# Three of every four FFN-up pairs by seven half-size products, with new orders on all queues

## The chip, the cores and the metric

The kernel runs on one core of one Trainium2 chip. The metric is the device time of one execution in microseconds (us), as the median of timed runs. A further execution is taken by the hardware profiler; all rows shown here come from it.

## The reference

Four layers are computed on a sequence of 512 tokens of width 1024. Each layer has a mixer (sliding-window attention, a gated MLP, sparse attention, sliding-window attention again) and a feed-forward part with a causal convolution of width 3 over the tokens. Only the feed-forward part is touched:

```python
def conv_ffn(x, w_up, conv_w, conv_b, w_down):
    h = x @ w_up                       # [512, 1024] @ [1024, 2 * 2816]
    ch = h.shape[-1]
    h = lax.conv_general_dilated(h, conv_w[:, None, :], window_strides=(1,), padding=((CONV_WIDTH - 1, 0),), ...) + conv_b
    gate, val = jnp.split(h, 2, axis=-1)
    return (jax.nn.silu(gate) * val) @ w_down
```

## The kernel before

The engines run separate programs, written out by hand and coupled by semaphores; each engine works its own list strictly in order. Everything is in fp32, and TensorE gets every operand as a high part and a low part (`hi`, and `lo` = value minus `hi`), with three matmuls for one product: hi by hi, hi by lo, lo by hi. ScalarE makes high parts by a copy, VectorE low parts by a subtraction.

The up projection has 44 weight slabs of 128 x 1024 per layer, two for each of 22 pairs: slab (q, 0) gives the gate rows of pair q, slab (q, 1) the value rows. An **ordinary pair** is two calls of `forward`, each 24 matmuls of 512 columns. A **seven-product pair** computes the same by Winograd's form of Strassen's scheme: the two slabs, cut in halves, are the 2 x 2 blocks of the weights, and seven products of 12 matmuls of 256 columns replace eight. It needs sums of weight blocks beforehand: x1, x2, x3 on VectorE (in place in the `raw` slots, x2 in one shared place, `sum_place`), and a fourth, x4, which POOL adds by an accumulating DMA (`fourth_sum`) and which has to land before the next pair's x2. It needs corrections in PSUM afterwards: c11, c22, c12 on VectorE, from three copies that ScalarE takes (`copy(q, 0..2)`). In TensorE's order the products are numbered 1, 2, 6, 5, 7, 4, 3. Product 6 waits for the first copy, product 7 for the second, product 4 for c22, product 1 for the low part a11, product 3 for x4.

After the matmuls every slab gets three convolution **taps**: one on ScalarE (`tap`, `fast_tap`), two on VectorE (`slab_taps`); then a silu on ScalarE and a `gate` on VectorE. Slabs are loaded by DMAs from SP's queue into four `raw` slots; the slot of (q, 1) comes free when the low parts x3 and x4 of pair q-2 are made. POOL also makes five sums per two pairs for the down projection (`down_sums`).

In each layer pairs 4, 6, 8, ... 16 are seven-product pairs, each followed by an ordinary one whose two slabs lie inside it: slab (q+1, 0) between products 7 and 4, slab (q+1, 1) after product 3. That is `period(q)` on ScalarE and VectorE, 21 us long. Pairs 0 to 3 and 18 to 21 are ordinary.

Of the kernel before, what the change touches and what calls it, by code (L numbers as in the profile page):

```python
# [10 lines left out]
SEQ = 512  # L11
DEPTH = 4
# [23 lines left out]
FASTS = (FAST_END - FAST) // 2  # L36
# [37 lines left out]
def build(nc, slabs, x_in, gains, conv, sinks, rel_bias, onehot, wsT, ln_g, ln_b, b_s, kv_g, kidx_g, out):  # L74
# [9 lines left out]
    with ExitStack() as ctx:  # L84
# [261 lines left out]
        def made(c):  # L346

            return loaded(c) - sum(up_slab(L, q, e) <= c for L in range(DEPTH) for q in range(FAST, FAST_END, 2) for e in range(2))
# [107 lines left out]
        def fast(L, q):  # L456

            return FASTS * L + (q - FAST) // 2

# [4 lines left out]
        def up_bank(q, e):  # L464

            return (0 if q // 2 % 2 else 4) + e
# [182 lines left out]
        def _(sp):  # L649
# [37 lines left out]
            for L, kind in enumerate(KINDS):  # L687
# [22 lines left out]
                for q in range(FAST, FAST_END + 2, 2):  # L710
                    for e in range(2):
                        c = up_slab(L, q, e)
                        if q == FAST:
                            sp.wait_ge(lo_made, made(c - RAW))
                        elif e:
                            sp.wait_ge(part_lo_made["x3"], fast(L, q - 2) + 1)
                            sp.wait_ge(part_lo_made["x4"], fast(L, q - 2) + 1)
                        else:
                            sp.wait_ge(part_lo_made["x1"], fast(L, q - 2) + 1)
                            sp.wait_ge(up_x2, fast(L, q - 2) + 1)  # L720
                            sp.wait_ge(up_x3, fast(L, q - 2) + 1)
                        sp.dma_start(raw[:, raw_slot(c), :], slabs[dram(c)]).then_inc(raw_in[raw_slot(c)], 16)
                    if q < FAST_END:
                        for e in range(2):
                            c = up_slab(L, q + 1, e)
                            sp.wait_ge(lo_made, made(c - RAW))
                            sp.dma_start(raw[:, raw_slot(c), :], slabs[dram(c)]).then_inc(raw_in[raw_slot(c)], 16)
# [14 lines left out]
        def _(pool):  # L742
# [80 lines left out]
            def down_sums(L, j):  # L823
# [5 lines left out]
                if j == 0:  # L829
                    pool.wait_ge(in_lo, 4 * (L + 1))  # L830
                pool.tensor_tensor(s1, a21, a22, ALU.add).then_inc(s_made, 1)  # L831
# [7 lines left out]
            def fourth_sum(L, q):  # L839

                pool.wait_ge(up_x2, fast(L, q) + 1)
                pool.wait_ge(part_lo_made["a11"], fast(L, q) + 1)
# [12 lines left out]
            for L, kind in enumerate(KINDS):  # L855
# [20 lines left out]
                fourth_sum(L, FAST)  # L876
                for j in range(STEPS - 1):
                    down_sums(L, j)
                    if FAST <= 2 * j + 4 < FAST_END and j:
                        fourth_sum(L, 2 * j + 4)  # L880
# [4 lines left out]
        def _(sc):  # L885
            squares = [0]

            def split_hi(c, i=0):
# [6 lines left out]
                if made(c) > RING:  # L895
                    sc.wait_ge(w_used, 4 * i + (c - (RING + EARLY if early(c - RING) else RING) + 1))
                if isinstance(i, int) and summed(c):
# [374 lines left out]
            def ffn_up(L, n0):  # L1272
# [11 lines left out]
                def fast_tap(q, e):  # L1284

                    sc.wait_ge(up_c, 3 * fast(L, q) + 2 + e)
                    if not e:
                        sc.wait_ge(up_mm, 5 * fast(L, q) + 4)
                        sc.wait_ge(gated, FFT * L + q - 1)
                    sc.wait_ge(neg_made, 1)  # L1290
                    scale = conv_sb[:, L, 2 * q + 1, 2:3] if e else conv_neg[:, L, (q - FAST) // 2, 2:3]
# [3 lines left out]
                def copy(q, n):  # L1295
# [3 lines left out]
                    else:  # L1299
                        sc.wait_ge(up_mm, 5 * fast(L, q) + (1, 3)[n])  # L1300
                    if q > FAST:
                        sc.wait_ge(up_c, 3 * fast(L, q - 2) + (1, 3, 2)[n])
                    sc.activation(kept_sum(n), ps[:, up_bank(q, 0), 0:HALF], ACT.Copy).then_inc(up_copy, 1)

                def part_hi(q, name):

                    even, odd = up_slab(L, q), up_slab(L, q, 1)
                    if name == "a11":
                        sc.wait_ge(raw_in[raw_slot(odd)], raw_count(odd))
                        if q > FAST:  # L1310
# [1946 lines left out]
```

## Time and profile before

| what | value |
|---|---|
| three timed runs | 2040.51, 2040.95, 2044.98 us; median 2040.95 |
| the profiled execution | 2042.29 us, span 2040.6 |
| busy: TensorE, weight loads | 2026.4 us (99%), 1750.7 (86%) |
| busy: VectorE, ScalarE, POOL | 1619.3 us (79%), 1115.0 (55%), 433.7 (21%) |
| granted TensorE clock | 1.00 (2.4 GHz) |
| chain that ended last | TensorE 91%, VectorE 5%, DMA 2%, ScalarE 1% |
| waits of TensorE for others | 2.4, 2.1, 1.2, 1.0, 0.6, 0.3, 0.3 us |

A busy time counts every instruction from start to end, also where two overlap in the pipeline. So the cost of an instruction in a dense stretch is the distance from its start to the next one's start, which is less than its own duration. The last row lists idle times that the profile can put down to another engine. In a row "x2" means two instructions merged, and a bracket at the end gives the idle time before it and what ended it.

### The profile page before, as it was taken

To read this page: it belongs to the slowest core of one execution; us is meant where nothing else is said; L and a number is where in the kernel's file an instruction comes from. 1 tells how busy PE (TensorE), PEld (TensorE's weight loads), DVE (VectorE), ACT (ScalarE), POOL (GpSimd) and SP (SyncE) were. 2 spreads that over 40 slices of the span, in tenths; PEclk is the share of its full clock that TensorE was granted. 3 is DMA by queue.
4 is the path that set the end of the run, shared out by engine and by line. 5 is a ranking of instruction groups with operands and counts; after the bars stand their busy time and mean duration, and the time that the engine had idled before them with its cause. 6 is when DMAs were issued, how large, how long until landed. Compare 5 with 4: busy or idle time off the path is not lost.

```text
span 2040.6 us, 33333 instructions
## 1 busy us (share of the span) xinstructions
PE 2026.4 (99%) x12636; PEld 1750.7 (86%) x12636; DVE 1619.3 (79%) x2555; ACT 1115.0 (55%) x1861; POOL 433.7 (21%) x482
## 2 busy tenths in 40 slices
PE   9999999999999999999999999999999999999998
PEld 8889998888988899888877888998888889999887
DVE  6668878889467887899888669777997668877898
ACT  4755545447335555546656646555465755545555
POOL 0520332210000232120035402322110520332220
PEclk9999999999999999999999999999999999999999
DMA  8123344384432334467421123334674122334393
GB/s 291 64 104 125 109 130 150 121 255 172 145 129 75 97 105 129 145 190 243 166 73 42 63 83 104 119 104 155 197 237 163 65 104 83 109 122 147 115 269 122
DMA packets 82570, 276.42 MB, mean 135 GB/s; under 512 B 9408, under 2 KB 13632, under 8 KB 82032
## 3 DMA queue, kind: packets, MB, share of 16 engines
q1 hardware_dynamic: 59184, 214.67, 30.4%
q0 software_dynamic: 11200, 24.12, 5.8%
q10 hardware_dynamic: 12032, 35.54, 4.8%
q8 instruction: 100, 1.64, 0.3%
q14 instruction: 54, 0.44, 0.1%
HBM read 256.43 MB, written 14.73 MB: 133 GB/s over the span
## 4 chain that ended last, share of the span: by engine, by line
PE 91%; DVE 5%; DMA 2%; ACT 1%; issue 0%; DVEq 0%; ACTq 0%; SPq 0%
PE ps L2437 12%; PE ps L2438 12%; PE ps L2439 12%; PE ps L2649 6%; PE ps L3018 5%; PE ps L3019 5%; PE ps L3020 5%; PE ps L2976 5%; PE ps L2978 5%; PE ps L2977 5%; PE ps L2509 2%; PE ps L2465 2%; PE ps L2466 2%; PE ps L2467 2%; DMA raw<-slabs 2%; PE ps L2497 1%
## 5 line engine op out<-in xcount | busy, mean ns | idle before, releaser
L2437 PE MATMUL ps<-h_hi,w_hi 128*128 128x512 f32 (+1 forms) x1104 | 433.0, 392 | 0.0
L2438 PE MATMUL ps<-h_lo,w_hi 128*128 128x512 f32 (+1 forms) x1104 | 429.6, 389 | 0.0
L2439 PE MATMUL ps<-h_hi,w_lo 128*128 128x512 f32 (+1 forms) x1104 | 428.9, 389 | 0.0
L1603 DVE TENSOR_TENSOR w_lo<-raw,w_hi 128x1024 fp32r<-128x1024 f32 x300 | 372.0, 1247 | 39.1 <-ACT w_hi L901 35.5
L901 ACT ACTIVATE w_hi<-raw 128x1024 fp32r<-128x1024 f32 x312 | 326.4, 1053 | 133.1 <-DVE raw L2251 74.0
L2437 PEld LDWEIGHTS ps<-h_hi,w_hi 128*128 128x128 f32 x1104 | 207.6, 188 | 44.0 <-issue 4.0
L2439 PEld LDWEIGHTS ps<-h_hi,w_lo 128*128 128x128 f32 x1104 | 207.3, 188 | 43.2
L2438 PEld LDWEIGHTS ps<-h_lo,w_hi 128*128 128x128 f32 x1104 | 207.7, 188 | 38.9
L1281 ACT ACTIVATE work<-ps,conv_sb 128x512 f32<-128x512 f32 x120 | 93.0, 775 | 162.6 <-PE ps L2439 133.2
L3018 PE MATMUL ps<-w_hi,h_hi 128*128 128x512 f32 x408 | 159.7, 391 | 2.1 <-DVE w_lo L1603 2.1
L3020 PE MATMUL ps<-w_hi,h_lo 128*128 128x512 f32 x408 | 158.8, 389 | 0.0
L3019 PE MATMUL ps<-w_lo,h_hi 128*128 128x512 f32 x408 | 158.8, 389 | 0.0
L831 POOL TENSOR_TENSOR bias<-act 128x256 f32<-128x256 f32 x40 | 65.9, 1647 | 410.3 <-DVE act L2146 410.3
L1332 ACT ACTIVATE w_hi<-raw 128x1024 fp32r<-128x1024 f32 (+1 forms) x84 | 77.1, 918 | 136.6 <-DMA raw<-slabs 82.0
L2040 DVE SCALAR_TENSOR_TENSOR work<-ps,conv_sb,work 128x511 f32<-128x511 f32 (+1 forms) x184 | 134.8, 745 | 3.2
L843 POOL DMA_DIRECT2D raw<-act x28 | 24.6, 877 | 507.7 <-DVE w_lo L2064 507.7
L2027 DVE SCALAR_TENSOR_TENSOR work<-ps,conv_sb,work 128x511 f32<-128x511 f32 (+1 forms) x112 | 77.4, 741 | 27.4 <-ACT work L1281 27.4
L2064 DVE TENSOR_TENSOR w_lo<-raw,w_hi 128x1024 fp32r<-128x1024 f32 (+1 forms) x84 | 89.3, 1063 | 11.9 <-ACT w_hi L1332 11.9
L2977 PE MATMUL ps<-h_lo,w_hi 128*128 128x256 f32 x336 | 95.1, 283 | 0.0
L2978 PE MATMUL ps<-h_hi,w_lo 128*128 128x256 f32 x336 | 95.1, 283 | 0.0
L2976 PE MATMUL ps<-h_hi,w_hi 128*128 128x256 f32 x336 | 94.9, 283 | 0.0
L3018 PEld LDWEIGHTS ps<-w_hi,h_hi 128*128 128x128 f32 x408 | 76.6, 188 | 19.4 <-issue 3.9
(365 smaller groups left out, 5054.6 us busy)
## 6 DMA issues: line engine op xcount, KB each, us to landing
raw<-slabs SPq DMA_DIRECT2D x368, 512.0 KB, 4.1
act<-slabs POOLq DMA_DIRECT2D x64, 256.0 KB, 5.6
bias<-slabs SPq DMA_DIRECT2D x16, 512.0 KB, 6.3
x_dram<-x ACTq DMA_DIRECT2D x16, 512.0 KB, 5.0
x<-x_dram ACTq DMA_DIRECT2D x16, 512.0 KB, 4.9
raw<-act POOLq DMA_DIRECT2D x28, 256.0 KB, 3.3
act<-slabs SPq DMA_DIRECT2D x12, 512.0 KB, 5.4
bias_dram<-bias_rows ACTq DMA_DIRECT2D x2, 2048.0 KB, 12.3
```

What stands on the lines that cost most here:

```text
L901: sc.activation(w_hi[:, c % RING, :], raw[:, raw_slot(c), :], ACT.Copy).then_inc(hi_made, 1)
L1603: ve.tensor_tensor(w_lo[:, c % RING, :], raw[:, raw_slot(c), :], w_hi[:, c % RING, :].bitcast(f32), ALU.subtract).then_inc(lo_made, 1)
L2040: ve.scalar_tensor_tensor(y, ps[:, bank, 0:SEQ - sh], scale, y, ALU.mult, ALU.add).then_inc(done, 1)
L2437: pe.matmul(ps[:, bank, cols], hi, h_hi[:, k, cols], start=k == 0, stop=False)
L2438: pe.matmul(ps[:, bank, cols], hi, h_lo[:, k, cols], start=False, stop=False)
L2439: last = pe.matmul(ps[:, bank, cols], lo, h_hi[:, k, cols], start=False, stop=k == KT - 1)
L2976: pe.matmul(o, hi[:, w], b_hi[:, k, :], start=begin and k == 0, stop=False, skip_group_check=onto)
L2977: pe.matmul(o, hi[:, w], b_lo[:, k, :], start=False, stop=False, skip_group_check=onto)
L2978: last = pe.matmul(o, lo[:, w], b_hi[:, k, :], start=False, stop=k == KT // 2 - 1, skip_group_check=onto)
L3018: pe.matmul(ps[:, bank, :], hi[at], w_hi[:, s, cols], start=begin, stop=False, skip_group_check=onto)
L3019: pe.matmul(ps[:, bank, :], hi[at], w_lo[:, s, cols], start=False, stop=False, skip_group_check=onto)
L3020: return pe.matmul(ps[:, bank, :], lo[at], w_hi[:, s, cols], start=False, stop=end, skip_group_check=onto)
```

## The change

Ten pairs per layer are done by seven products instead of seven: 4, then 6, 7, 8, then 10, 11, 12, then 14, 15, 16. Pairs 5, 9, 13 and 17 stay ordinary. Pair 4 with the ordinary pair 5 forms the first period (`first_period(4)`); a group is `period(f)` for f = 6 and 10 and `last_period(14)`, which runs on into pairs 18 to 21 and the first sums of the down projection. Each engine's order is written out anew, tap by tap. Pairs inside the fast part use four pairs of PSUM banks in turn, where the ordinary ones used two. The waits count by name of pair and product. The shortened diff:

```diff
+FAST_RUNS = 6, 10, 14
+IN_GROUP = 3
+FAST_PAIRS = [FAST] + [q + e for q in FAST_RUNS for e in range(IN_GROUP)]
...
         def up_bank(q, e):
-            return (0 if q // 2 % 2 else 4) + e
+            return 2 * ((q + 2) % 4 if FAST <= q < FAST_END else q % 2) + e
...
+                load_pair(FAST)
+                load_pair(FAST + 1)
+                for f in FAST_RUNS:
+                    load(f, 0)
+                    load(f + 1, 0)
+                    load(f, 1)
+                    load(f + 1, 1)
+                    load(f + 2, 0)
+                    load(f + 2, 1)
+                    load(f + 3, 0)
+                    load(f + 3, 1)
...
-                fourth_sum(L, FAST)
-                for j in range(STEPS - 1):
+                fourth_sum(L, 4)
+                down_sums(L, 0, 4)
+                fourth_sum(L, 6)
+                down_sums(L, 1, 6)
+                fourth_sum(L, 7)
+                fourth_sum(L, 8)
+                down_sums(L, 2, 8)
...
+            def down_sums(L, j, landed=None):
...
+                if landed:
+                    pool.wait_ge(up_x4, 16 * (fast(L, landed) + 1))
...
                     if q > FAST:
                         ve.wait_ge(part_lo_made["x2"], fast(L, q))
+                        ve.wait_ge(up_x3, fast(L, q))
                         ve.wait_ge(up_x4, 16 * fast(L, q))
...
+                for f in FAST_RUNS:
+                    p1(f)
+                    p2(f)
+                    p6_p5(f)
+                    p1(f + 1)
+                    p7(f)
+                    p2(f + 1)
+                    p4(f)
+                    p3(f)
+                    p6_p5(f + 1)
+                    p7(f + 1)
+                    p1(f + 2)
+                    p4(f + 1)
+                    p2(f + 2)
+                    p3(f + 1)
+                    p6_p5(f + 2)
+                    p7(f + 2)
+                    bank_free(f + 3)
+                    forward(up_slab(L, f + 3), 0, up_bank(f + 3, 0))
+                    p4(f + 2)
+                    p3(f + 2)
+                    forward(up_slab(L, f + 3, 1), 0, up_bank(f + 3, 1))
```

The scheduled places that the next sections speak of are three. First TensorE, whose rows carry their waits. Before, pair 6 from product 5 on; L2976 is the first matmul of a product, L2437 that of an ordinary slab, and x1_lo, x3_lo, x4_lo and a11_lo are the low parts:

```order
L2976 MATMUL ps<-g_post_r,w_hi 128x256 [waits x1_lo]
...
L2976 MATMUL ps<-x_r,a_hi 128x256 [waits x3_lo,up_copy]
...
L2437 MATMUL ps<-h_hi,w_hi 128x512 [waits lo_made,tap0]
...
L2976 MATMUL ps<-x_r,w_hi 128x256 [waits up_c]
...
L2976 MATMUL ps<-h_hi,w_hi 128x256 [waits x4_lo]
...
L2437 MATMUL ps<-h_hi,w_hi 128x512 [waits lo_made]
...
L2976 MATMUL ps<-h_hi,w_hi 128x256 [waits a11_lo,tap0]
```

After, pair 6 from product 5 on and pair 7 among it (L3270 is the first matmul of a product):

```order
L3270 MATMUL ps<-g_post_r,w_hi 128x256 [waits x1_lo]
...
L3270 MATMUL ps<-h_hi,w_hi 128x256 [waits a11_lo,tap0]
...
L3270 MATMUL ps<-x_r,a_hi 128x256 [waits x3_lo,up_copy]
...
L3270 MATMUL ps<-x_r,w_hi 128x256 [waits up_c]
...
L3270 MATMUL ps<-h_hi,w_hi 128x256 [waits x4_lo]
...
L3270 MATMUL ps<-work_r,a_hi 128x256 [waits in_lo,x2_lo,up_copy]
...
L3270 MATMUL ps<-g_post_r,w_hi 128x256 [waits x1_lo]
...
L3270 MATMUL ps<-x_r,a_hi 128x256 [waits x3_lo,up_copy]
...
L3270 MATMUL ps<-h_hi,w_hi 128x256 [waits a11_lo,tap0]
...
L3270 MATMUL ps<-x_r,w_hi 128x256 [waits up_c]
```

What moved: products 7 and 4 of pair 6, and of pair 7, have only one product of another pair between them (product 2 of pair 7, without a wait of its own, and product 1 of pair 8), where an ordinary slab stood.

Second ScalarE in the first period, up to the two taps that end it. Before; L1332 is a high part, L1292 the tap of a seven-product slab, L1378 the silu, L1281 the tap of an ordinary slab, and L1303 a copy:

```order
L1332 ACTIVATE w_hi<-raw 128x1024
L1332 ACTIVATE a_hi<-act 128x512
L1292 ACTIVATE work<-ps,conv_sb,conv_neg 128x512
L1332 ACTIVATE w_hi<-raw 128x1024
L1292 ACTIVATE work<-ps,conv_sb 128x512
L1378 ACTIVATE work<-work 128x512
L1281 ACTIVATE work<-ps,conv_sb 128x512 x2
```

After (L1394 a high part, L1353 a tap, L1551 the silu, L1364 a copy):

```order
L1394 ACTIVATE w_hi<-raw 128x1024 x2
L1394 ACTIVATE a_hi<-act 128x512
L1353 ACTIVATE work<-ps,conv_sb,conv_neg 128x512
L1394 ACTIVATE w_hi<-raw 128x1024
L1394 ACTIVATE a_hi<-raw 128x512
L1551 ACTIVATE work<-work 128x512
L1394 ACTIVATE w_hi<-raw 128x1024
L1353 ACTIVATE work<-ps,conv_sb 128x512
L1364 ACTIVATE bias<-ps 128x256
```

What moved: high parts for two coming pairs stand around the first tap, and the silu, the high part a11 of pair 7 and a tap stand ahead of the first copy of pair 6, the last row. At the period's start, not in these rows, `copy(4, 0)` now comes ahead of the high part x3 of pair 4 and behind the high part of slab (5, 0).

Third VectorE in the first period, from the split of slab (5, 0) on. Before; L1603 is a split of an ordinary slab, L2146 a gate, L2047 and L2052 are c11 and c22, L2064 a low part, L2071 the sum x1 and L2088 the sum x2:

```order
L1603 TENSOR_TENSOR w_lo<-raw,w_hi 128x1024
L2146 TENSOR_TENSOR act<-work 128x512
L1603 TENSOR_TENSOR w_lo<-raw,w_hi 128x1024
L2047 TENSOR_TENSOR ps<-ps,bias 128x256
L2064 TENSOR_TENSOR w_lo<-raw,w_hi 128x512
L2052 TENSOR_TENSOR ps<-ps,act 128x256
L2071 TENSOR_TENSOR raw<-raw 128x512
L2088 TENSOR_TENSOR act<-raw 128x512
```

After (L1755 a split, L2190 a tap, L2226 x1, L2465 a gate, L2202 c11, L2219 a low part, L2207 c22, L2244 x2):

```order
L1755 TENSOR_TENSOR w_lo<-raw,w_hi 128x1024
L2190 SCALAR_TENSOR_TENSOR work<-ps,conv_sb,work 128x511
L2190 SCALAR_TENSOR_TENSOR work<-ps,conv_sb,work 128x510
L2226 TENSOR_TENSOR raw<-raw 128x512
L2465 TENSOR_TENSOR act<-work 128x512
L1755 TENSOR_TENSOR w_lo<-raw,w_hi 128x1024
L2226 TENSOR_TENSOR raw<-raw 128x512
L2202 TENSOR_TENSOR ps<-ps,bias 128x256
L2219 TENSOR_TENSOR w_lo<-raw,w_hi 128x512
L2207 TENSOR_TENSOR ps<-ps,act 128x256
L2244 TENSOR_TENSOR act<-raw 128x512
```

What moved: the split comes ahead of the taps of slab (3, 1), and two sums x1, of pairs 6 and 7, stand ahead of the low part x4 of pair 4, the row before c22; the load of slab (6, 1) waits for that low part.

## Rows read from the trace of the kernel before

**Rows 1.** Waits of TensorE over the span, longest first
```profile
PE ps L3160 <- POOL same_tile L751: 2.4, 1, 2.4
```

**Rows 2.** One window: length, busy us of PE, PEld, DVE, ACT, POOL, PEclk, DMA
```profile
247.00:289.00 42.00, 42.00 (x265) 38.17 (x264) 32.95 (x47) 21.78 (x32) 11.91 (x12) 1.00 0.37 114
```

**Rows 3.** Timeline of TensorE, starts of products and slabs (start, us, engine, line)
```profile
205.36 0.28 PE L2976 MATMUL ps<-h_hi,w_hi 128*128 128x256 f32 x1
...
226.47 0.28 PE L2976 MATMUL ps<-h_hi,w_hi 128*128 128x256 f32 x1
...
233.66 0.40 PE L2437 MATMUL ps<-h_hi,w_hi 128*128 128x512 f32 x1
...
239.13 0.28 PE L2976 MATMUL ps<-x_r,w_hi 128*128 128x256 f32 x1
...
242.00 0.40 PE L2437 MATMUL ps<-h_hi,w_hi 128*128 128x512 f32 x1
...
247.47 0.28 PE L2976 MATMUL ps<-h_hi,w_hi 128*128 128x256 f32 x1
```

**Rows 4.** Timeline of ScalarE, first copy of pair 4
```profile
207.82 0.37 ACT L1303 ACTIVATE bias<-ps 128x256 f32<-128x256 f32 x1
```

**Rows 5.** Timeline of VectorE, first period of the first layer
```profile
209.37 1.52 DVE L2040 SCALAR_TENSOR_TENSOR work<-ps,conv_sb,work 128x511 f32<-128x511 f32 x2
...
218.33 0.69 DVE L2088 TENSOR_TENSOR act<-raw 128x512 f32<-128x512 f32 x1 [1.92 <-issue]
219.37 1.22 DVE L2064 TENSOR_TENSOR w_lo<-raw,w_hi 128x1024 fp32r<-128x1024 f32 x1 [0.35 <-ACT w_hi L1332]
220.51 0.68 DVE L2064 TENSOR_TENSOR a_lo<-act,a_hi 128x512 fp32r<-128x512 f32 x1
221.11 1.53 DVE L2040 SCALAR_TENSOR_TENSOR work<-ps,conv_neg,work 128x511 f32<-128x511 f32 x2
222.55 0.42 DVE L2058 TENSOR_TENSOR ps<-ps,bias 128x256 f32<-128x256 f32 x1
222.88 1.22 DVE L2064 TENSOR_TENSOR w_lo<-raw,w_hi 128x1024 fp32r<-128x1024 f32 x1
...
225.46 0.68 DVE L2078 TENSOR_TENSOR raw<-act,raw 128x512 f32<-128x512 f32 x1
226.06 0.68 DVE L2146 TENSOR_TENSOR act<-work 128x512 f32<-128x512 f32 x1
```

**Rows 6.** Timeline of ScalarE, then VectorE: third copy of pair 8, then c22
```profile
254.86 0.38 ACT L1303 ACTIVATE act<-ps 128x256 f32<-128x256 f32 x1 [0.75 <-PE ps L2978]
...
255.27 0.43 DVE L2052 TENSOR_TENSOR ps<-ps,act 128x256 f32<-128x256 f32 x1 [0.44 <-ACT act L1303]
```

**Rows 7.** Timeline of the load queue, second slab of pair 6
```profile
214.98 0.33 SPq L722 DMA_DIRECT2D raw<-slabs  x1
```

**Rows 8.** Timeline of ScalarE, first period of the first layer
```profile
218.27 1.06 ACT L1332 ACTIVATE w_hi<-raw 128x1024 fp32r<-128x1024 f32 x1 [5.03 <-DMA raw<-slabs]
219.24 0.61 ACT L1332 ACTIVATE a_hi<-act 128x512 fp32r<-128x512 f32 x1
...
223.01 0.78 ACT L1292 ACTIVATE work<-ps,conv_sb 128x512 f32<-128x512 f32 x1 [0.69 <-DVE ps L2058]
223.69 0.62 ACT L1378 ACTIVATE work<-work 128x512 f32<-128x512 f32 x1
224.21 0.77 ACT L1281 ACTIVATE work<-ps,conv_sb 128x512 f32<-128x512 f32 x1
```

**Rows 9.** Timeline of POOL, fourth sum of pair 6
```profile
221.16 0.88 POOL L843 DMA_DIRECT2D raw<-act  x1 [3.34 <-DVE w_lo L2064]
```

**Rows 10.** The page, part 6: fourth sums, KB each, us to landing
```profile
raw<-act POOLq DMA_DIRECT2D x28, 256.0 KB, 3.3
```

**Rows 11.** Lines L2071 and L832: ns min/median/max, first and last start
```profile
L2071 DVE TENSOR_TENSOR raw<-raw x28: 681/724/1252, 197.5 to 1852.9; 128x512 f32<-128x512 f32 x28
...
L832 POOL COPY vbuf<-act x32: 388/920/929, 207.8 to 1872.4; 128x256 f32<-128x256 f32 x32
```

More of the change, by code:

```diff
@@ L346, in made @@
         def made(c):
-            return loaded(c) - sum(up_slab(L, q, e) <= c for L in range(DEPTH) for q in range(FAST, FAST_END, 2) for e in range(2))
+            return loaded(c) - sum(up_slab(L, q, e) <= c for L in range(DEPTH) for q in FAST_PAIRS for e in range(2))
         def raw_slot(c):
@@ L709, in _, with load @@
                 ring_slabs(n1 + EARLY, up_slab(L, FAST))
[L710 to L727, printed above, removed]
+                def load(q, e):
+                    c = up_slab(L, q, e)
+                    if q - 2 not in FAST_PAIRS:
+                        sp.wait_ge(lo_made, made(c - RAW))
+                    elif e:
+                        sp.wait_ge(part_lo_made["x3"], part_count(L, q - 2, "x3"))
+                        sp.wait_ge(part_lo_made["x4"], part_count(L, q - 2, "x4"))
+                    else:
+                        sp.wait_ge(part_lo_made["x1"], part_count(L, q - 2, "x1"))
+                        sp.wait_ge(up_x2, fast(L, q - 2) + 1)
+                        sp.wait_ge(up_x3, fast(L, q - 2) + 1)
+                    sp.dma_start(raw[:, raw_slot(c), :], slabs[dram(c)]).then_inc(raw_in[raw_slot(c)], 16)
@@ L1375, in silu, with slab_silu @@
+                def slab_silu(q):
+                    silu(q % 2, q // 2)
                 def silu(c, i):
@@ new lines, in first_period @@
+                def first_period(f):
+                    split_lo(up_slab(L, f + 1))
+                    slab_tap(f - 1, 1, 1)
+                    slab_tap(f - 1, 1, 0)
+                    x1(f + 2)
+                    slab_gate(f - 1)
+                    split_lo(up_slab(L, f + 1, 1))
+                    x1(f + 3)
+                    c11(f)
+                    part_lo(f, "x4")
+                    c22(f)
+                    x2(f + 2)
+                    part_lo(f + 2, "a11")
+                    part_lo(f + 3, "x1")
+                    x3(f + 2)
+                    part_lo(f + 2, "x2")
+                    part_lo(f + 2, "x1")
+                    slab_tap(f, 0, 1)
+                    x2(f + 3)
+                    slab_tap(f, 0, 0)
+                    part_lo(f + 2, "x3")
+                    c12(f)
+                    part_lo(f + 3, "a11")
+                    slab_tap(f, 1, 1)
+                    x3(f + 3)
+                    slab_tap(f, 1, 0)
+                    slab_tap(f + 1, 0, 1)
+                    slab_gate(f)
+                    c11(f + 2)
+                    x1(f + 4)
+                    part_lo(f + 2, "x4")
+                    slab_tap(f + 1, 0, 0)
+                    part_lo(f + 3, "x2")
+                    c22(f + 2)
@@ L2143, in gate, with slab_gate @@
+                def slab_gate(q):
+                    gate(q % 2, q // 2)
                 def gate(c, i):
```

580 lines of the change are left out of this document (405 added, 175 removed).

## The prediction

> **What bounds the kernel now.** I read the waits of TensorE first, then the starts of its matmuls over one pair of FFN slabs, then VectorE and ScalarE in the same stretch. TensorE waits almost nowhere: its longest wait of the whole span is 2.4 us, in the set-up, before the first layer [rows 1]. In the stretch from 247 us, TensorE is busy for 42.00 of 42.00 us at the full granted clock (2.4 GHz), VectorE for 32.95 and ScalarE for 21.78 [rows 2]. So the time is TensorE's own work, and only a change of that work, or a new wait on it, moves the end.
>
> The starts in [rows 3] price that work. The first five products of a seven-product pair run from 226.47 to 233.66: 7.19 us, 1.44 each. An ordinary slab then runs to 239.13 (5.47), two products to 242.00 (2.87), another ordinary slab to 247.47 (5.47). A seven-product pair costs 7.19 + 2.87 = 10.06 us and an ordinary pair 10.94, together 21.00. The period before it took 205.36 to 226.47 = 21.11; the 0.11 is a small wait for the copy that ends at 208.19 [rows 3, 4], in front of the third product of pair 4.
>
> **The change on TensorE.** Per layer the seven-product pairs go from 7 (4, 6, ... 16) to 10. Six ordinary slabs go (6 x 5.47 = 32.82) and 21 products come (21 x 1.437 = 30.18): 2.64 us, 10.6 over four layers. The copy that pair 4 waited for goes ahead of the high part of the third sum, so the 0.11 goes too: 0.4 over four layers. With no new wait the sum is -11.0 us.
>
> One rule of the Trainium skill speaks against the change. At 2.4 GHz, [rows 3] give 228 ns for a matmul of 512 columns (5.47 / 24) and 120 for one of 256 (1.44 / 12). The page "TensorE: Matmul & The Clock Gate", section "Back-to-back issue gap", puts a sustained stream at about 131 ns for 512 columns, and an isolated gap at N/2.4 + 2.5, which is 216 and 109. By 131 an ordinary pair would cost 48 x 0.131 = 6.3 us, and each conversion would lose nearly 4; by the isolated gap each would win 10.36 - 9.18 = 1.18, 14 in all. The rows are this very stream, and they decide against both.
>
> **VectorE.** Its prices are the distances between starts in [rows 5]: a low part of 1024 columns 1.14 (219.37 to 220.51), of 512 columns 0.60, two taps 1.44, a correction in PSUM 0.33 (222.55 to 222.88), a sum or a gate 0.60 (225.46 to 226.06). A new group of three seven-product pairs and one ordinary one needs 16 taps (11.5), 8 low parts or splits of 1024 (9.1), 9 low parts of 512, 9 sums and 4 gates (22 x 0.60 = 13.2) and 9 corrections (3.0): 36.8 us. TensorE's group is 3 x 10.06 + 10.94 = 41.1. The same count for two old periods is 32.2, against 32.95 busy. VectorE goes from 78% to 90% and stays below TensorE, with 4.3 us of slack a group. ScalarE gains three high parts and three copies per converted pair, and has twice the room.
>
> Cover, though, gets thin. Formerly an ordinary slab (5.47) stood between the seventh product and the fourth; now, for the first two pairs of a group, one product (1.44). In between lie the copy and the correction c22: the seventh product ends at 254.66 (233.66 + 21.00), the copy starts at 254.86, c22 at 255.27 and ends at 255.70 [rows 6]. That is 1.04 of 1.44, if both engines are free just then. I laid the new order of a whole group against TensorE's clockwork in this way, one instruction after the other with these prices and the waits in the code. ScalarE and VectorE are free there, since both have just done the x4 parts, which become ready 1.4 us earlier. The a11 low parts come 1.5 to 2.5 us ahead of their products, the split of an ordinary slab 1.8. Weight loads take 3.3 us from the issue at 214.98 to the high part at 218.27 [rows 7, 8] and are issued 5 or more ahead. On POOL, five sums for the down projection now stand in front of the fourth sum of a group's second pair; at some 1 us each, like POOL's copy [rows 11], they take about 5 us, and the x4 behind them is wanted 9 us later. I take 0 for the groups. The bounds: nothing, and about 0.5 a group (6 us), should the 0.4 left at c22 be missed by that much; VectorE's contention with POOL is the likeliest reason, below.
>
> **The first period** of a layer (pairs 4 and 5) does not fit so well. VectorE is free at 209.37 [rows 5]. Its new order is split 1.14, two taps 1.44, x1 0.60, gate 0.60, split 1.14, x1 0.60, c11 0.33, low part x4 0.60, with 0.2 for the longer x4 seen there: done near 216.0. That releases the load of the second slab of pair 6, which was issued at 214.98 [rows 7], so the two sums x1 moved ahead of it make it 1.0 late. It lands 3.3 later, at 219.3. Then, on the chain: high part, and 1.10 after its start the low part a11 (as 218.27 to 219.37 [rows 5, 8]) at 220.4; two low parts 2.28, x3 0.60, low x2 0.60, low x1 1.14, tap 0.72, x2(7) 0.60, tap 0.72: 227.06. The x2(7) at 225.7 also needs the fourth sum of pair 6; POOL issues that 0.6 after the low part a11 (221.16 after 219.37 + 1.22 [rows 5, 9]), and it takes 3.3 [rows 10], so 225.4: just in time. ScalarE has queued behind that tap the silu 0.52 (223.69 to 224.21), the high part a11(7) 0.97 (218.27 to 219.24), the tap of slab (4,1) 0.68 (223.01 to 223.69) [rows 8], and only then the first copy of pair 6 (0.37, as in [rows 4]): done near 229.7. The third product of pair 6 is due at 226.36 + 2.87 = 229.23. It waits 0.5 us; four layers give 2.0. The bounds of this term: 0, if the chain runs 0.5 faster, and 1.5 a layer (6.0), if POOL's down sums, which now begin only when the fourth sum of pair 4 has landed, stretch VectorE's sums as they stretched one x1 to 1.25 from a median of 0.72 [rows 11].
>
> **Last period.** Pairs 18 to 21 keep their TensorE work. VectorE's list from the correction of pair 14 to the gate of pair 21 sums to about 69 us by the same prices, TensorE has 71.5 from product 3 of pair 14 to its last slab, and the last taps wait for the last slab as before. I take 0.
>
> **Sum.** -10.6 - 0.4 + 2.0 = -9.0. The profiled execution took 2042.29 (span 2040.6, the rest lies around it), so it would be 2033.3; it lay 1.3 above the median of the three timed runs, 2040.95. On the median: 2032.
>
> **Rivals.** *A, small waits in the groups.* VectorE's sums and POOL's compete: L2071 ranges from 681 to 1252 ns, POOL's copy from 388 to 929 with a median of 920 [rows 11]. A denser VectorE meets POOL more often. At 0.2 to 1 us in each of 12 groups the time is 2034.4 to 2044, centre 2039, about no change. Against it: [rows 2] hold two rounds of POOL's sums and VectorE's busy time is within 0.8 of the sum of undisturbed prices. The Trainium skill, "SBUF — State Buffer", says that a VectorE instruction with two SBUF inputs and a GpSimd one that reads SBUF exclude each other for a whole instruction; by that rule each meeting could cost up to a POOL sum's length, and the trace shows stretched rows but mostly smaller ones.
>
> *B, slower: VectorE's chain becomes the bound of the group.* Each seven-product pair has a serial chain: x4's low part, load, x2, a11, fourth sum, x4. In the old order VectorE stood idle 1.92 us for the load [rows 5]. If each of the three pairs still costs 2 us idle, 36.8 + 6 = 42.8 exceeds 41.1 by 1.7; the gain of a group is 0.88, so it turns at 42.0. Twelve groups lose 20: 2052. Against it: the new order puts other pairs' taps into that hole.
>
> *C, no wait in the first period:* 2030, on the forecast's own side.
>
> **How the numbers follow.** Changes within 0.2% (4 us) can't be told from none here. The forecast with C: 0.62, all faster. A: 0.24, of which 0.11 faster and 0.13 same. B: 0.10, slower. Something not listed, 0.04, split evenly between faster and same. That gives 0.75, 0.15, 0.10. The range goes from 2029.5 (the full sum of -11.0, half a us below) to 2038.5 (the groups' bound of 6 on top of the forecast); outside lie B and the upper part of A, some 0.2.
>
> **What would show it.** The starts of the first products of pairs 6, 10 and 14 should lie 41.1 us apart. A gap of about 0.5 before the third product of pair 6, ended by ScalarE's copy, shows the first-period term. VectorE should be near 37 of 41 us busy. The weight load that waits for x4(4) should be issued near 216.0. The forecast is wrong if the groups take more than 41.3 us, if TensorE's waits name VectorE's corrections or low parts in every group, or if the down projection starts to wait for its low parts.

## The result and the profile after

The change makes the kernel slower. Its median is 2053.64 us (2051.67 to 2056.84, four runs), beside 2040.73 for the kernel before on the same chip: a ratio of 1.0064, 95% interval 1.0052 to 1.0076. Forecast was 2032 with a range up to 2038.5. The profiled execution took 2054.36, span 2052.3, against 2042.29 and 2040.6 before: 11.75 us more.

The waits of TensorE come first again, over the whole span of the changed kernel (total, times, longest). They answer to [rows 1].

```profile
PE ps L3270 <- ACT bias L1364: 8.8, 4, 2.9
PE ps L3356 <- DVE w_lo L1755: 4.1, 5, 1.5
PE ps L3498 <- POOL same_tile L788: 2.4, 1, 2.4
...
PE ps L3270 <- DVE ps L2207: 0.8, 2, 0.4
```

The first line is new: four waits, one a layer, for ScalarE's first copy (L1364). It is the place that the forecast named, but 2.2 us where it had 0.5. The second is the down projection, waiting for low parts; the last is c22.

Next the starts of TensorE's matmuls in layer 0: pair 4, pair 6, the wait, then pairs 10, 14 and 18. They answer to [rows 3].

```profile
206.14 0.28 PE L3270 MATMUL ps<-h_hi,w_hi 128*128 128x256 f32 x1
...
227.14 0.28 PE L3270 MATMUL ps<-h_hi,w_hi 128*128 128x256 f32 x1
...
229.89 0.28 PE L3272 MATMUL ps<-h_hi,w_lo 128*128 128x256 f32 x1
232.23 0.38 PE L3270 MATMUL ps<-work_r,a_hi 128*128 128x256 f32 x1 [2.06 <-ACT bias L1364]
...
272.10 0.28 PE L3270 MATMUL ps<-h_hi,w_hi 128*128 128x256 f32 x1
...
313.41 0.28 PE L3270 MATMUL ps<-h_hi,w_hi 128*128 128x256 f32 x1
...
355.11 0.39 PE L2731 MATMUL ps<-h_hi,w_hi 128*128 128x512 f32 x1
```

Pairs 4 and 5 take 227.14 - 206.14 = 21.00: the 0.11 is gone, as forecast. The first group takes 44.96 us, the second 41.31, the third 41.70. Against a pace of 41.16, which a run below shows for a group without any wait, that is 3.80, 0.15 and 0.54 too much. From 229.89 to 232.23 are 2.34 us where 0.12 is the pitch: a gap of 2.22. The other 1.6 us that the first group has too much lie behind it. Three windows show this (length, busy us of PE, PEld, DVE, ACT, POOL, granted clock, DMA share, GB/s): the stretch of [rows 2] in the new kernel, the wait, and the 3.41 us behind it.

```profile
247.00:289.00 42.00, 42.00 (x308) 39.98 (x307) 39.77 (x57) 24.43 (x40) 13.03 (x13) 1.00 0.43 120
229.50:233.20 3.70, 1.64 (x14) 1.44 (x13) 3.00 (x5) 3.54 (x6) 3.62 (x5) 1.00 0.21 85
233.25:236.66 3.41, 3.41 (x18) 3.41 (x17) 2.86 (x5) 1.17 (x3) 1.10 (x2) 0.50 0.44 77
```

Behind the wait the granted clock is 0.50, which is 1.2 GHz, and 256-column matmuls start 213 ns apart instead of 120. VectorE is now busy for 39.77 of 42.00 us, against 32.95 before. Over the second group alone, and below it over the same group of a kernel with small down sums (a run below), the rows are (columns as above)

```profile
272.10:313.26 41.16, 41.16 (x301) 39.17 (x300) 39.17 (x56) 23.76 (x38) 12.88 (x13) 1.00 0.43 122
266.19:307.35 41.16, 41.16 (x302) 39.25 (x301) 36.97 (x56) 23.64 (x38) 7.13 (x13) 1.00 0.43 122
```

The forecast's 36.8 us a group was right for a VectorE beside small sums (36.97); beside the full sums it is busy for 2.2 more (39.17).

### The profile page after: what moved, and what is told of

Same layout as the page of the kernel before. It is cut to its first block and busy times, and to the rows that moved or that the text cites. A ratio compares the mean times of both kernels' runs of the same rounds, so it can differ in the third digit from the quotient of the medians.

```text
span 2052.3 us, 34572 instructions
## 1 busy us (share of the span) xinstructions
PE 2026.7 (99%) x13068; PEld 1769.8 (86%) x13068; DVE 1681.1 (82%) x2666; ACT 1138.4 (55%) x1933; POOL 446.4 (22%) x494
## 5 line engine op out<-in xcount | busy, mean ns | idle before, releaser
L1755 DVE TENSOR_TENSOR w_lo<-raw,w_hi 128x1024 fp32r<-128x1024 f32 x276 | 349.9, 1276 | 40.5 <-ACT w_hi L957 37.3
L2731 PE MATMUL ps<-h_hi,w_hi 128*128 128x512 f32 (+1 forms) x912 | 358.3, 393 | 0.3 <-DVE w_lo L1755 0.2
L2732 PE MATMUL ps<-h_lo,w_hi 128*128 128x512 f32 (+1 forms) x912 | 354.7, 389 | 0.0
L2733 PE MATMUL ps<-h_hi,w_lo 128*128 128x512 f32 (+1 forms) x912 | 354.3, 389 | 0.0
L2731 PEld LDWEIGHTS ps<-h_hi,w_hi 128*128 128x128 f32 x912 | 171.4, 188 | 37.8 <-issue 4.0
L2732 PEld LDWEIGHTS ps<-h_lo,w_hi 128*128 128x128 f32 x912 | 171.5, 188 | 32.4
L2190 DVE SCALAR_TENSOR_TENSOR work<-ps,conv_sb,work 128x511 f32<-128x511 f32 x224 | 164.4, 740 | 25.2 <-ACT work L1353 24.3
L1394 ACT ACTIVATE w_hi<-raw 128x1024 fp32r<-128x1024 f32 (+1 forms) x120 | 108.9, 914 | 117.2 <-DMA raw<-slabs 55.5
L2219 DVE TENSOR_TENSOR w_lo<-raw,w_hi 128x1024 fp32r<-128x1024 f32 (+1 forms) x120 | 137.0, 1145 | 13.3 <-ACT w_hi L1394 13.3
L3270 PE MATMUL ps<-h_hi,w_hi 128*128 128x256 f32 x480 | 135.8, 283 | 0.0
L3271 PE MATMUL ps<-h_lo,w_hi 128*128 128x256 f32 x480 | 135.8, 283 | 0.0
L3272 PE MATMUL ps<-h_hi,w_lo 128*128 128x256 f32 x480 | 135.8, 283 | 0.0
L1353 ACT ACTIVATE work<-ps,conv_sb 128x512 f32<-128x512 f32 x112 | 86.3, 775 | 84.2 <-PE ps L2733 84.2
L3270 PEld LDWEIGHTS ps<-h_hi,w_hi 128*128 128x128 f32 x480 | 92.1, 192 | 0.8 <-issue 0.2
L3271 PEld LDWEIGHTS ps<-h_lo,w_hi 128*128 128x128 f32 x480 | 92.1, 192 | 0.6
```

The costliest lines, as they stand in the source:

```text
L1755: ve.tensor_tensor(w_lo[:, c % RING, :], raw[:, raw_slot(c), :], w_hi[:, c % RING, :].bitcast(f32), ALU.subtract).then_inc(lo_made, 1)
L2190: ve.scalar_tensor_tensor(y, ps[:, up_bank(q, e), 0:SEQ - sh], scale, y, ALU.mult, ALU.add).then_inc(done, 1)
L2731: pe.matmul(ps[:, bank, cols], hi, h_hi[:, k, cols], start=k == 0, stop=False)
L2732: pe.matmul(ps[:, bank, cols], hi, h_lo[:, k, cols], start=False, stop=False)
L2733: last = pe.matmul(ps[:, bank, cols], lo, h_hi[:, k, cols], start=False, stop=k == KT - 1)
L3270: pe.matmul(o, hi[:, w], b_hi[:, k, :], start=begin and k == 0, stop=False, skip_group_check=onto)
```

## Where the wait comes from

TensorE waits for ScalarE, ScalarE for VectorE's tap, and that whole chain started with a slab that came late. Rows of VectorE, then POOL, then the load queue, then ScalarE, in layer 0 of the changed kernel; they answer to [rows 5, 9, 7, 8].

```profile
212.57 0.83 DVE L2226 TENSOR_TENSOR raw<-raw 128x512 f32<-128x512 f32 x1
213.32 1.22 DVE L2465 TENSOR_TENSOR act<-work 128x512 f32<-128x512 f32 x1
214.47 1.75 DVE L1755 TENSOR_TENSOR w_lo<-raw,w_hi 128x1024 fp32r<-128x1024 f32 x1
216.15 0.68 DVE L2226 TENSOR_TENSOR raw<-raw 128x512 f32<-128x512 f32 x1
...
209.98 1.83 POOL L870 TENSOR_TENSOR bias<-act 128x256 f32<-128x256 f32 x1 [2.65 <-DMA raw<-act]
...
212.81 1.18 POOL L874 TENSOR_TENSOR act<-bias,act 128x256 f32<-128x256 f32 x1
...
217.83 0.81 SPq L746 DMA_DIRECT2D raw<-slabs  x2
...
221.91 2.01 ACT L1394 ACTIVATE w_hi<-raw 128x1024 fp32r<-128x1024 f32 x2 [8.00 <-DMA raw<-slabs]
...
229.66 0.63 ACT L1551 ACTIVATE work<-work 128x512 f32<-128x512 f32 x1 [3.03 <-DVE work L2190]
230.20 1.04 ACT L1394 ACTIVATE w_hi<-raw 128x1024 fp32r<-128x1024 f32 x1
231.14 0.76 ACT L1353 ACTIVATE work<-ps,conv_sb 128x512 f32<-128x512 f32 x1
231.81 0.37 ACT L1364 ACTIVATE bias<-ps 128x256 f32<-128x256 f32 x1
```

Read the distances between starts. The gate takes 214.47 - 213.32 = 1.15 where the forecast had 0.60, the split 216.15 - 214.47 = 1.68 instead of 1.14, the first x1 0.75 instead of 0.60. All three run while POOL makes its down sums (from 209.98), and POOL's own sums are longer too (1.83 and 1.18). So slab (6,1) is asked for at 217.83, which is 11.69 behind pair 4's first product; the forecast had 10.64. Its high part begins at 221.91, 4.08 after the request, where [rows 7, 8] had 3.29. From there ScalarE's queue goes as priced, with silu, high part and tap ahead of the first copy, and that ends at 232.18.

Two theories, then. *Theory 1:* POOL's sums stretch VectorE's work, that shifts the request, and the order on ScalarE hands all of it on to TensorE. *Rival:* the sums are harmless, and the slab's landing or the queues' own length hold the wait. A second question is what the groups and the down projection lose by themselves.

## The experiments

Each kernel was timed in five rounds beside the kernel before, which gave 2041.25 in the first comparison, 2040.65 in the second and 2040.68 in the third (23 to 29 runs each). "Expected" is the text that was on record before the run.

**First copy of pair 6 ahead of the queue** (ScalarE, `first_period`):

```diff
+                    copy(f + 2, 0)
                     slab_silu(f)
                     part_hi(f + 3, "a11")
                     slab_tap(f, 1)
-                    copy(f + 2, 0)
```

> Only ScalarE's order in the first period changes: the first copy of pair 6 goes ahead of the silu of pair 4, the high part a11 of pair 7 and the tap of slab (4,1). Theory (the copy is late because of what is queued ahead of it on ScalarE, and the long wait it causes also lets TensorE's clock fall): the wait before product 6 of pair 6, 2.2 to 3.1 us a layer, goes away, and the stretch at 1.2 GHz behind it with it. VectorE is then late next: its correction c22 of pair 6 comes 1.5 to 2 us after product 4 could start, so a wait of that size moves there. Net 2043 to 2049. Rival (VectorE as a whole is the bound, the place of the wait is chance): all of the wait comes back further on, and the time stays at 2052 or more.

Measured 2048.74 us, ratio 1.0037 (1.0024 to 1.005). The largest entry among its waits of TensorE:

```profile
PE ps L3270 <- DVE ps L2207: 8.0, 7, 1.7
```

The wait for the copy is gone, and a wait for c22 (L2207) stands in its place, 1.84 us in each layer, before product 4 of pair 6, five products later: VectorE has its own queue ahead of c22. In this execution the clock did not fall. Most of the stall was moved, not removed.

**The same, with c22 of pair 6 ahead of x1, tap and low parts** (VectorE):

```diff
+                    c22(f + 2)
+                    part_lo(f + 2, "x4")
                     x1(f + 4)
-                    part_lo(f + 2, "x4")
                     slab_tap(f + 1, 0, 0)
                     part_lo(f + 3, "x2")
-                    c22(f + 2)
```

> The same, and on VectorE c22 of pair 6 goes ahead of the sum x1 of pair 8, a tap and two low parts. Theory: neither wait is left in the first period, no stretch at 1.2 GHz is left, 14 us less than the changed kernel: 2038 to 2042. Rival (VectorE is the bound): at best as the run with the copy alone, 2047 or more, with new waits in pairs 7 and 8.

Measured 2039.66 us, ratio 0.9997 (0.9988 to 1.0005): 12 to 14 us below the changed kernel. The edit moves more than the copy and c22: the low part x4 of pair 6 goes ahead of x1 with it, and the run doesn't tell its share. The clock does not fall in the profile. The largest wait left in the first groups is 0.8 us between starts, in layer 3, for the low part a11 of pair 7; those for c22 are small.

```profile
PE ps L3270 <- DVE ps L2207: 1.3, 3, 0.4
```

**The last tap of pair 21 ahead of the operand copy** (ScalarE, `last_period`):

```diff
                     split_hi(DOWN[L] + 2)
+                    slab_tap(f + 7, 1)
                     operand(L, 3)
                     slab_silu(f + 7)
-                    slab_tap(f + 7, 1)
```

> Only the end of ScalarE's list of the up projection changes: the tap of the last slab goes ahead of an operand's high part and a silu. Theory (VectorE enters the down projection 1.0 us later than before because of that tap, and where VectorE needs 5.5 us a step for TensorE's 5.44 the lost lead comes back as waits): VectorE's last split starts 3.0 us after the down projection's start instead of 4.0, and the waits for splits there fall from 4.1 us to some 2; 2051 to 2052. Rival (those waits are the loads' or chance): no change, 2053.6.

Measured 2047.1 us, ratio 1.0032 (1.002 to 1.0045). VectorE makes the last split 3.43 us after the start of the down projection instead of 3.99 (2.99 in the kernel before), and small waits of 0.16 us (0.44 in layer 2) just behind it are gone, 0.9 in all. The down projection's other waits did not fall in the profiled execution, which was the slowest of the five: they are 5.1 us in all, where the text expected 2 instead of 4.1. The time fell by more than the 1.6 to 2.6 us expected, 6.5 against the first median of the changed kernel and 4.7 against the second (below), whose interval overlaps with this one. So the time moved as the theory has it, and the waits that were to show why did not.

**Down sums small.** POOL's five sums work on 8 of their 256 columns; the rest of the down projection's sums is left out.

```diff
+                s1, kept, s4 = s1_place(j)[:, 0:8], pa_place(j)[:, 0:8], pa_place(j)[:, HALF:HALF + 8]
+                a21, a11, a22, a12 = (part[:, 0:8] for part in (a21, a11, a22, a12))
```

> POOL's sums for the down projection run on 8 of 256 columns, so most of their work is left out; every wait and increment stays. Theory (POOL's sums stretch VectorE's low parts and sums, which makes the x4 low part and so the load of slab (6,1) late and eats the cover of c22): VectorE's stretched rows (1.2 us for 0.68) vanish, the wait before product 6 of pair 6 falls from 2.2 to 3.1 us to some 1.2, the clock doesn't fall behind it, the waits for c22 go: 2040 to 2045. Rival (contention with POOL is small change, the orders alone are at fault): 2051 or more.

Measured 2039.77 us, ratio 0.9994 (0.9985 to 1.0002). The first-period wait is 0.8 to 1.5 us, the clock does not fall behind it, and every second and third group takes 41.16 us. This fits theory 1, but it takes out work as well as contention. The profiled execution was the slowest of eleven (2044.58), with waits of 6.6 us for low parts in the down projection; the median is the better guide to the time.

**The changed kernel once more**, unchanged, in the second comparison:

> The changed kernel, unchanged, timed once more beside the others as the base of their differences. Both theories expect 2053 us (2050 to 2056), 1.006 of the kernel before.

Measured 2051.84 us (2046.52 to 2052.62), ratio 1.005 (1.0036 to 1.0063). The four waits for the copy are there again (2.15, 1.98, 2.24 and 2.80 us). What varies is the clock. Two windows of this profile lie at the wait of layer 3 and behind it:

```profile
1770.30:1773.40 3.10, 0.46 (x5) 0.26 (x3) 2.63 (x4) 2.66 (x5) 3.02 (x5) 1.00 0.21 86
1773.50:1776.90 3.40, 3.40 (x30) 3.40 (x30) 3.40 (x6) 2.35 (x5) 1.82 (x2) 1.00 0.33 58
```

That is a wait of 2.8 us without a fall behind it.

**The same sums, later.** All work is kept; only the first five sums of a layer wait for pair 4's low part x4:

```diff
+                if low:
+                    pool.wait_ge(part_lo_made["x4"], part_count(L, low, "x4"))
...
-                down_sums(L, 0, 4)
+                down_sums(L, 0, low=4)
```

> GpSimd's first five down sums of a layer wait for the low part of pair 4's fourth sum, so they run from about 11 us after pair 4's first product (where VectorE waits for slab (6,1)) and not from 3.6 us. Theory 1 (beside these sums VectorE's gate, split, x1 run 0.4 to 0.6 us longer each, so slab (6,1) is asked for 1.05 us late, and the wait before product 6 of pair 6 reaches 2.2 us, behind which the clock falls in three layers): the request goes out near 10.7 us after the pair's start, the wait is about 1.2 us, no clock fall behind it, sum 2053 - 4 x 1.0 - 3 x 1.45 = about 2045 us. Rival 2 (the 4.0 us that the slab takes to land, and ScalarE's queue, hold the wait; the sums' neighbours have slack): wait 2.0 us or more, clock falls as before, 2053 us.

Measured 2043.45 us, ratio 1.0012 (1.0003 to 1.0021): 8.4 below the changed kernel, as theory 1 has it. VectorE's rows, then POOL's first, the loads and ScalarE's high part:

```profile
211.05 0.68 DVE L2467 TENSOR_TENSOR act<-work 128x512 f32<-128x512 f32 x1
211.65 1.22 DVE L1757 TENSOR_TENSOR w_lo<-raw,w_hi 128x1024 fp32r<-128x1024 f32 x1
212.79 0.69 DVE L2228 TENSOR_TENSOR raw<-raw 128x512 f32<-128x512 f32 x1
...
214.59 0.73 POOL L872 TENSOR_TENSOR bias<-act 128x256 f32<-128x256 f32 x1 [9.37 <-DVE w_lo L2221]
...
214.48 0.80 SPq L746 DMA_DIRECT2D raw<-slabs  x2
...
218.61 1.06 ACT L1396 ACTIVATE w_hi<-raw 128x1024 fp32r<-128x1024 f32 x1 [6.81 <-DMA raw<-slabs]
```

The gate is back at 0.60, the split at 1.14, and POOL's sum at 0.73 instead of 1.83. Pair 4 starts at 204.02 here, so the request goes out after 10.46 us and not 11.69. The wait is 0.8 to 1.0 us in each layer, with no fall of the clock behind it. What did not go is the landing: 4.13 us (3.87 to 3.93 in the other layers).

**The second load apart from the first**, on top of the later sums:

```diff
                     load(f, 1)
+                    if f == FAST_RUNS[0]:
+                        sp.wait_ge(part_hi_made["a11"], part_count(L, f, "a11"))
                     load(f + 1, 1)
```

> On top of the later down sums, the load of slab (7,1) is not issued 0.37 us behind that of (6,1) but once the high part a11 of pair 6 has been read out of the landed (6,1). Theory 1 (two slabs in flight share the queues, which is why (6,1) lands 3.9 to 4.1 us after its issue and not 3.3): (6,1)'s high part starts near 13.8 us after pair 4's first product and not at 14.3 to 14.6, the wait before product 6 of pair 6 falls from 0.9 to about 0.3 us, 2043.4 - 4 x 0.6 = 2041 us. Rival 2 (a load in this stretch takes 4 us by itself): the high part starts at 14.3 to 14.6 as before, 2043 us, or above if (7,1) now comes late.

Measured 2042.51 us, ratio 1.0008 (0.9999 to 1.0017). The loads and the high part (pair 4 starts at 203.91):

```profile
214.36 4.85 SPq L746 DMA_DIRECT2D raw<-slabs  x2
...
217.79 2.01 ACT L1398 ACTIVATE w_hi<-raw 128x1024 fp32r<-128x1024 f32 x2 [6.11 <-DMA raw<-slabs]
```

The landing is 3.43 us (3.44 to 3.54 in the other layers), near the 3.29 of [rows 7, 8], and the wait falls from 0.8 to 1.0 us to 0.33 to 0.44 in three layers, as theory 1 expected; in layer 3 it stays at 1.09, because x2 of pair 7 starts 0.7 us later there than in the other layers. In the times the difference is 0.9 us, less than the 2.4 expected and not more than the uncertainty.

**Three reorderings together:** the early copy and c22 of pair 6, the early last tap, the later first sums. No new code beyond the diffs above.

> Three reorderings together: the first copy of pair 6 ahead of the SiLU of pair 4 on ScalarE and the sum c22 of pair 6 early on VectorE (run before: 2039.7), the last period's tap ahead of the operand copy, and the first down sums later as in the run with them alone. Theory 1 (what is left above the forecast are first-period and group waits of 0.3 to 0.6 us and VectorE's lost lead at the down projection): 2039.7 - 4 x 0.3 (first period) - 4 x 0.4 (down projection) = about 2037 us, which would be below the kernel before. Rival 2 (the down projection's waits are set by the landing of its slabs, the first period is at its floor already): 2039.7, the same as the kernel before.

Measured 2035.6 us (2033.17 to 2039.79, eleven runs), ratio 0.9978 (0.9969 to 0.9987). It is the fastest kernel here with all of the work, 5.1 below the kernel before. Waits of TensorE, then starts of pairs 6, 10, 14 and 18 in layer 0:

```profile
PE ps L3272 <- DVE ps L2209: 0.8, 2, 0.4
PE ps L3358 <- DVE w_lo L1757: 0.7, 2, 0.4
...
226.44 0.28 PE L3272 MATMUL ps<-h_hi,w_hi 128*128 128x256 f32 x1
...
267.60 0.28 PE L3272 MATMUL ps<-h_hi,w_hi 128*128 128x256 f32 x1
...
308.90 0.28 PE L3272 MATMUL ps<-h_hi,w_hi 128*128 128x256 f32 x1
...
350.20 0.39 PE L2733 MATMUL ps<-h_hi,w_hi 128*128 128x512 f32 x1
```

The first group takes 41.16, here and in all four layers: its wait is gone. The other two take 41.30 here, and 41.3 to 42.4 elsewhere.

**The same with small down sums** (left out as above):

> The early copy and c22 of pair 6 and the last period's tap order, and GpSimd's down sums over 8 of their 256 columns (the down projection's sums are left out but for these, so this kernel computes something else in its down projection). If GpSimd's sums beside VectorE are what keeps the groups from their products' pace (theory 1), the waits for c22 and for low parts in the groups fall under 0.1 us each, the fast part reaches -2.75 us a layer, 2040.7 - 11 + down projection = 2030 to 2033 us. If the groups' waits have another source (rival: VectorE's and ScalarE's own queues), about 2037 us as with all sums at full size.

Measured 2033.45 us, half a us above what theory 1 expected, ratio 0.9965 (0.9956 to 0.9975). Starts of pairs 6, 10, 14 and 18 in layer 0:

```profile
225.03 0.28 PE L3271 MATMUL ps<-h_hi,w_hi 128*128 128x256 f32 x1
...
266.19 0.28 PE L3271 MATMUL ps<-h_hi,w_hi 128*128 128x256 f32 x1
...
307.35 0.28 PE L3271 MATMUL ps<-h_hi,w_hi 128*128 128x256 f32 x1
...
348.50 0.39 PE L2732 MATMUL ps<-h_hi,w_hi 128*128 128x512 f32 x1
```

Three times 41.16 (41.15 by rounding). Eleven of twelve groups take this, one 41.22. So the groups' remaining waits need POOL's sums at full size, and 41.16 is TensorE's own pace: seven products of 1.44 three times, and 10.92.

**First copy of pair 4 back behind the third sum's high part**, in the kernel with three reorderings:

```diff
-                    copy(f, 0)
                     part_hi(f, "x3")
+                    copy(f, 0)
```

> The three reorderings together, with one part of the change undone: the first copy of pair 4 stands behind the high part of the third sum again, as in the kernel before. By the forecast's term the wait of 0.11 us before the third product of pair 4 comes back in each layer, and nothing else: 2035.6 + 0.4 = 2036 us. Rival: the small wait hid nothing, since later work has slack for it: 2035.6; or the high part x3 was what the order is for and TensorE gains elsewhere by it: below 2035.

Measured 2036.89 us, ratio 0.9981 (0.9973 to 0.999). Pairs 4 and 5 take 21.11, 21.11, 21.11 and 21.10 us instead of 21.00 in the four layers, and the groups behind start just as before. This part of the change is worth 0.43 us, as forecast; the times can't show so little. This kernel has the early last tap too. In its profiled execution (2037.49 us) TensorE waits for low parts in the down projection, and VectorE for slabs in layer 1 (from 820 to 990 us), like this:

```profile
PE ps L3358 <- DVE w_lo L1757: 4.2, 3, 2.0
...
DVE raw L2539 <- DMA raw<-slabs: 3.9, 2, 2.2
```

**Without the early last tap**, other reorderings kept:

> The three reorderings without that of the last period's tap. If VectorE's lead at the start of the down projection (1.0 us less than in the kernel before, and 0.4 to 0.6 of it back with the tap's order) decides the down projection's waits, they rise again: w_lo waits of 3 to 7 us in all, 2035.6 + 2 to 4 = about 2038.5 us. Rival (those waits come from slabs that land late, by chance in one execution and not in another): 2035.6, and waits within what the runs of other kernels show.

Measured 2040.08 us (2035.94 to 2044.76, twelve runs), ratio 0.9996 (0.9986 to 1.0006), 4.5 above the kernel with all three and 3.2 above the one with the first copy of pair 4 back. The profiled execution was one of its two lowest. In it TensorE waits 2.7 us for low parts in the down projection, less than the 3 to 7 expected. What VectorE waits for in layer 1, from 820 to 940 us:

```profile
DVE raw L2539 <- DMA raw<-slabs: 3.2, 3, 1.9
```

The times speak for "lead decides"; the rival (chance alone) would have had 2035.6. The profiles can't settle it. With the early tap the same waits of TensorE are 0.7 us in one kernel and 4.2 in the next, without it 2.7, and slabs of the down projection land late for VectorE either way, by up to 1.9 us here and 2.2 with the tap. So one execution says little here, and by what path the tap gives its 3 to 4.5 us is not shown. The time is also the same as that of this kernel without later sums (2039.66). The traces do show a gain from these: the first groups take 41.16 us four times, against 41.55, 41.35, 41.49 and 42.03 without, 1.8 us in all, which the times are too coarse to confirm.

## Why the prediction was wrong, point by point

The starts split the profiled difference of 11.75 us without a rest. Before pair 4 of layer 0 and between the layers: +0.8 (it varies by 1 to 2 us from execution to execution). From pair 4 to the down projection the kernel before needs 190.63, 190.61, 190.63 and 190.63 us, the changed one 192.49, 192.95, 191.57 and 192.88: +7.4. The down projections: +3.5.

| term, four layers | forecast | measured |
|---|---|---|
| conversion, 12 groups | -10.6 | 12 x (41.16 - 42.00) = -10.1 |
| first copy of pair 4 | -0.4 | -0.4 |
| wait before product 6 of pair 6 | +2.0 | 2.22 + 2.13 + 2.07 + 3.07 = +9.5 |
| slower clock behind that wait | none | +4.8 |
| other waits in the groups | 0 | +3.6 |
| pairs 18 to 21 | 0 | 0 (43.52 us from pair 18 to the down projection in each layer of both) |
| down projection | 0 | +3.5 |
| ahead of the layers' pair 4 | 0 | +0.8 |

The sum on the right is +11.7, against a forecast of -9.0. Of the 20.7 us between them, 12.3 are the first-period wait and the slower clock behind it, 3.6 the groups and 3.5 the down projection.

**TensorE's arithmetic held.** The conversion came out at 0.84 a group instead of 0.88. The rule that spoke against it, in the Trainium skill's page "TensorE: Matmul & The Clock Gate", "Back-to-back issue gap", a sustained stream at about 131 ns for 512 columns, is not what happens in this stream, which takes 227 to 228 ns.

**The step that failed** is the first period: "It waits 0.5 us; four layers give 2.0", with 1.5 a layer as the bound. Place, cause of the wait and the engines on the chain were right. In layer 0 the wait was 2.22. Of the 1.7 too little, 1.05 is the late request, since the forecast took VectorE's durations undisturbed while POOL's down sums, which the changed order puts just there, ran beside them. It had named this as a bound, by one x1 in [rows 5, 11], and chose against it. The later sums take 1.2 us off the request and 8.4 off the time. Another 0.8 is the landing, 4.08 and not 3.29; the rest of the chain ran 0.1 faster. The 3.29 was the price of that one load, 3.20 to 3.29 in all four layers of the kernel before. The forecast carried it over to a changed order of loads without a bound, though the page of the kernel before has a longer median over all slab loads, from issue to landing:

```profile
raw<-slabs SPq DMA_DIRECT2D x368, 512.0 KB, 4.1
```

Setting the second load apart gives 3.43 back, so its neighbour lengthens it. That can't be all: in the kernel before, two more loads were issued 0.4 and 0.85 us behind the one of [rows 7], and it took 3.29. What makes the difference is open. In layer 3 the fourth sum of pair 6 landed late as well, 4.19 us after its issue instead of 3.3 ("just in time" in the forecast); the wait there is 0.85 longer than in layer 0.

**No term for the clock.** Three waits of 2.13 to 3.07 us had 3.4 us at a granted clock of 0.50 behind them, which cost 1.6 us each. The Trainium skill's page "TensorE: Matmul & The Clock Gate", Part 1, says that half rate is the default state and that activity releases it; the rows agree as to the two levels, 0.50 and 1.00. A forecast wait of 0.5 us gave no reason to count it, a bound of 1.5 should have.

**The groups.** "I take 0 for the groups" was 3.6 too little, within its bounds of 0 to 6. The mechanism is the one named there, VectorE beside POOL, with a second condition that the forecast did not have. Rows of VectorE in layer 1 of the changed kernel, in the third group; the first is x2 of pair 15, which waits for the fourth sum of pair 14:

```profile
808.19 0.69 DVE L2244 TENSOR_TENSOR act<-raw 128x512 f32<-128x512 f32 x1 [0.59 <-DMA raw<-act]
808.80 1.76 DVE L2219 TENSOR_TENSOR w_lo<-raw,w_hi 128x1024 fp32r<-128x1024 f32 x1
...
811.15 0.92 DVE L2219 TENSOR_TENSOR a_lo<-raw,a_hi 128x512 fp32r<-128x512 f32 x1
811.99 1.23 DVE L2233 TENSOR_TENSOR raw<-act,raw 128x512 f32<-128x512 f32 x1
813.14 1.22 DVE L2219 TENSOR_TENSOR w_lo<-raw,w_hi 128x512 fp32r<-128x512 f32 x1
...
815.28 0.41 DVE L2207 TENSOR_TENSOR ps<-ps,act 128x256 f32<-128x256 f32 x1
```

Operations of 0.68 take 0.92 to 1.23, one of 1.22 takes 1.76, and c22 comes 0.67 us too late for product 4. With small sums the group is at its pace.

What tells the slow groups from the others is that first row. In the second and third groups of the changed kernel this x2 waits for the fourth sum just three times, 0.59 us (third group, layer 1), 0.92 and 0.31 (second and third, layer 2), and these groups are 1.12, 1.00 and 0.41 us above 41.16. Of the five without such a wait four are 0.11 to 0.15 above it and one 0.54 (third group, layer 0), where TensorE waits for a split. In the kernel with three reorderings and small sums the same waits of x2 are there (0.57, 0.90 and 0.78), and the groups take 41.22, 41.16 and 41.16. So the traces say that it takes both, a late fourth sum and the stretched rows behind it. Why the sum lands late in just these groups stays open.

Rival A (2034.4 to 2044) had this mechanism and its size; by itself it would have ended near 2035.5. It did not have the first period, where the same mechanism did the larger harm. The Trainium skill's page "SBUF — State Buffer", "SBUF: two separate sides", has a VectorE instruction with two SBUF inputs and a GpSimd one that reads SBUF exclude each other for a whole instruction. The runs agree that both sides wait (gate +0.55, POOL's sum 1.83 against 0.73), and each VectorE instruction lost at most 0.55, less than one undisturbed sum of POOL.

**Rival B**, VectorE as the bound of every group, was wrong: it put the loss at the right total (2052) for a wrong reason. Groups two and three never took more than 42.4 us in any run; in the changed kernel four of the eight took 41.3.

**The down projection** lost 3.5 us where the forecast had looked only as far as its start ("the last taps wait for the last slab as before"). TensorE reaches it in the same 43.52 us, but the new order has ScalarE do the operand copy and a silu ahead of the last tap, so VectorE makes its last split 1.0 us later. The kernel before, too, waits 2.1 us for low parts there; the changed one waits 4.1. The early tap gives 4.5 us in one pair of kernels, 3.2 in another, and 4.7 to 6.5 against the two medians of the changed kernel. That the late split lets late slabs through to TensorE is the likely path and not shown: TensorE's waits for low parts there are 0.7 to 5.1 us in the four profiles with the early tap and 2.7 to 7.1 in the eight without.

## What to carry to other kernels

A reordered kernel changes which instructions run side by side: lay the other engines' new start times beside each row of the critical chain, and take the contended price (VectorE beside GpSimd's sums: +0.55 us for each of two or three operations; a load with another 0.4 us behind it: some 0.4 to 0.8 us more, in this kernel) where they overlap. When a wait is found, look for the instruction that TensorE needs and what stands ahead of it in each queue, one engine after the other: moving the copy alone moved the wait to VectorE, moving c22 and the low part x4 as well gave 12 us. A stall of 2 us can cost 3.5, because the clock may fall behind it.

## What the hardware showed that was not expected

The fall of the clock behind a wait is not a matter of the wait's length alone. In two executions of the same kernel it followed waits of 2.13, 2.15, 2.22, 2.24 and 3.07 us, and did not follow waits of 1.98, 2.07 and 2.80. In the run with the early last tap, whose first period is the same, it followed 2.38, 1.92 and 3.13 us and not 2.11. POOL's sum of 256 columns ran 1.83 us instead of 0.73 beside VectorE, so the loss is on both sides. The load of slab (6,1) took 3.7 to 4.2 us from request to use in all layers of the eleven profiles that have a second load 0.4 us behind it, 3.4 to 3.5 us with that one held back, and 3.2 to 3.3 in the kernel before with two behind it.
